# Two mixer networks in one kernel: the last third of every feed-forward made the short one, the handover between phases reordered, and GpSimd's four subtractions merged into one

## The reference, cut to what matters

```python
for l in range(DEPTH):                       # DEPTH = 2
    lat = lat + 0.5 * ml[2] * _swiglu(_modulate(lat, norm_ffn1_g[l], ml[0], ml[1]), *ffn1)
    cx = cx + 0.5 * mc[2] * _swiglu(_modulate(cx, norm_ffn1_g[l], mc[0], mc[1]), *ffn1)
    ... # token mixer on both, residual added
    lat = lat + 0.5 * ml[8] * _swiglu(_modulate(lat, norm_ffn2_g[l], ml[6], ml[7]), *ffn2)
def _swiglu(h, w1, w3, w2):                  # hidden width 2816 = 22 blocks of 128
    return (jax.nn.silu(h @ w1) * (h @ w3)) @ w2
def _modulate(x, g, shift, scale):
    return _rmsnorm(x, g) * (1 + scale) + shift
```

## Time and profile before

| | us |
|---|---|
| median of 3 runs | 2768.28 |
| the profiled execution, its own time | 2765.99 |
| its span, first to last instruction | 2764.2 |
| PE busy | 2650.8 (96%) |
| DVE busy | 1186.9 (43%) |
| ACT busy | 1099.7 (40%) |
| POOL busy | 879.5 (32%) |
| mean granted TensorE clock, share of full speed | 0.977 |

### The profile page before, as it was taken

One profiled execution on the slowest core, in us unless ns is written; L12 is line 12 of the kernel. 1 busy time (PEld: TensorE's weight loads), 2 busy tenths in 40 slices (PEclk: granted clock), 3 DMA queues, 4 the chain that ended last, 5 costly groups with the idle time before them and its releaser, 6 DMA issues. The chain is left out here.

```text
span 2764.2 us, 44695 instructions
## 1 busy us (share of the span) xinstructions
PE 2650.8 (96%) x17377; PEld 2352.3 (85%) x17377; DVE 1186.9 (43%) x1774; ACT 1099.7 (40%) x1517; POOL 879.5 (32%) x1092
## 2 busy tenths in 40 slices
PE   6999999999999999999999999889999999997999
PEld 3777788988888877787877889879999999995999
DVE  3222324226652222252222247654447565634644
ACT  2322333534334222243122247536664554443533
POOL 0222221320013222222222216214544455540554
PEclk8999999999999999999999999999999999997999
DMA  6343542330024344323344334234544345450454
GB/s 236 133 165 131 174 145 92 138 122 16 32 77 160 130 144 152 137 92 137 137 142 147 137 115 154 76 112 151 188 167 150 140 157 188 175 181 16 168 183 152
DMA packets 58503, 376.49 MB, mean 136 GB/s; under 512 B 6223, under 2 KB 12007, under 8 KB 14216
## 3 DMA queue, kind: packets, MB, share of 16 engines
q1 hardware_dynamic: 56988, 371.51, 37.5%
q10 hardware_dynamic: 1388, 3.16, 0.7%
HBM read 370.44 MB, written 3.16 MB: 135 GB/s over the span
## 5 line engine op out<-in xcount | busy, mean ns | idle before, releaser
L1648 POOL TENSOR_TENSOR WL<-RAW,WH 128x256 fp32r<-128x256 f32 x1088 | 879.2, 838 | 1872.3 <-ACT WH L1197 1872.3
L1197 ACT ACTIVATE WH<-RAW 128x1024 fp32r<-128x1024 f32 x544 | 545.7, 1050 | 958.4 <-PE PSA L549 940.7
L1671 DVE TENSOR_TENSOR WL<-RAW,WH 128x1024 fp32r<-128x1024 f32 x272 | 338.2, 1243 | 1139.5 <-ACT WH L1197 1139.4
L547 PE MATMUL PSA<-HH,WH 128*128 128x512 f32 (+1 forms) x1664 | 598.8, 360 | 16.8 <-DVE HL L1756 7.9
L548 PE MATMUL PSA<-HL,WH 128*128 128x512 f32 (+1 forms) x1664 | 589.5, 354 | 0.0
L549 PE MATMUL PSA<-HH,WL 128*128 128x512 f32 (+1 forms) x1664 | 588.7, 354 | 0.0
L547 PE MATMUL PSA<-GH,WH 128*128 128x256 f32 (+1 forms) x1664 | 529.4, 318 | 4.8 <-DVE GL L1689 4.8
L548 PE MATMUL PSA<-GL,WH 128*128 128x256 f32 (+1 forms) x1664 | 521.4, 313 | 0.0
L549 PE MATMUL PSA<-GH,WL 128*128 128x256 f32 (+1 forms) x1664 | 521.0, 313 | 0.0
L547 PEld LDWEIGHTS PSA<-HH,WH 128*128 128x128 f32 x1664 | 316.3, 190 | 75.8 <-issue 25.7
L549 PEld LDWEIGHTS PSA<-HH,WL 128*128 128x128 f32 x1664 | 316.4, 190 | 43.8
(11 more groups left out here) (298 smaller groups left out, 3064.1 us busy)
## 6 DMA issues: line engine op xcount, KB each, us to landing
RAW<-in_weights SPq DMA_DIRECT2D x272, 1024.0 KB, 4.8
ADA<-in_w_ada SPq DMA_DIRECT2D x65, 1024.0 KB, 4.8
Zada<-in_w_ada SPq DMA_DIRECT2D x7, 1024.0 KB, 13.4
scratch_bias<-BREL ACTq DMA_DIRECT2D x1, 2048.0 KB
SUMS<-in_c_sums SPq DMA_DIRECT2D x1, 1664.0 KB, 8.5
TB<-scratch_bias SPq DMA_DIRECT2D x1, 1536.0 KB, 10.8
X<-in_x SPq DMA_DIRECT2D x1, 1024.0 KB, 8.4
X<-in_ctx SPq DMA_DIRECT2D x1, 1024.0 KB, 12.4
```

What stands on the lines that cost most here:

```text
L547: pe.matmul(out, a_hi, b_hi, start=start, stop=False)
L1197: act.activation(WH[:, j, 4 * h:4 * h + 4, :], RAW[:, j, 4 * h:4 * h + 4, :], ACT.Copy)\
L1648: ins = pool.tensor_tensor(WL[:, j, kb, :], RAW[:, j, kb, :], WH[:, j, kb, :].bitcast(F32), ALU.subtract)
L1671: dve.tensor_tensor(WL[:, j, 0:4, :], RAW[:, j, 0:4, :], WH[:, j, 0:4, :].bitcast(F32), ALU.subtract)\
```

## The change

`THIRDS` goes from (8, 6, 8) to (8, 8, 6). The number of slots and of matmuls stays the same; the `down` phase with 6 used blocks is now the last of each feed-forward. In the handover, PE does `part(2, 0)` whole before the column sums of stream 1; ACT splits the first of the next slots ahead of `root(1)`, and the second ahead of `high(1, 0)`; DVE evicts and splits earlier. POOL's four instructions per slot become one of four times the size.

```diff
--- before.py
+++ after.py
@@ -30,7 +30,7 @@
 NL = 256
 FF = 2816
 FFB = FF // P
-THIRDS = (8, 6, 8)
+THIRDS = (8, 8, 6)
 SLOT = KB * 256
 EPS = 1e-6
 NEG = -1.0e30
@@ -652,9 +652,9 @@
             def units_by_stream(ph):
 
                 kin = ph["kin"]
-                def part(u, s, ms=(0, 1)):
+                def part(u, s):
                     j, t = u % 2, streams(512)[s][1]
-                    for m in ms:
+                    for m in range(2):
                         w = slice(P * m, P * m + P)
                         for kb in range(kin):
                             if s == 1 and m == 0:
@@ -672,9 +672,8 @@
                 if has_ada(ph, 1):
                     ada_finish(ph, 1)
                 pe.wait_ge(bank_read[1], 2 + ph["unit"] + BANK_CREDIT)
-                part(2, 0, (0,))
+                part(2, 0).then_inc(mm_done, 1)
                 part_sums(3, 1)
-                part(2, 0, (1,)).then_inc(mm_done, 1)
                 part(3, 0).then_inc(mm_done, 1)
                 part_sums(2, 0)
 
@@ -1236,14 +1235,13 @@
                                        bias=MODS[:, ph["mods"][0], kb, s:s + 1]).then_inc(hh_ready, 1)
                 squares(2, 1)
                 squares(3, 1)
+                after_slot(down, 1, 0, 2)
                 root(1)
-                after_slot(down, 1, 0, 2)
                 squares(2, 0)
-                high(1, range(0, 3))
                 after_slot(down, 1, 1, 2)
-                high(1, range(3, 7))
+                high(1, range(0, 4))
                 squares(3, 0)
-                high(1, range(7, KB))
+                high(1, range(4, KB))
                 root(0)
                 high(0, range(KB))
 
@@ -1644,9 +1642,8 @@
 
             def split_lo(slot, j):
                 pool.wait_ge(hi_ready, slot * 2 + 2)
-                for kb in range(4, KB):
-                    ins = pool.tensor_tensor(WL[:, j, kb, :], RAW[:, j, kb, :], WH[:, j, kb, :].bitcast(F32), ALU.subtract)
-                ins.then_inc(lo_ready[1], 1)
+                pool.tensor_tensor(WL[:, j, 4:8, :], RAW[:, j, 4:8, :], WH[:, j, 4:8, :].bitcast(F32), ALU.subtract)\
+                    .then_inc(lo_ready[1], 1)
 
             for slot in range(2):
                 split_lo(slot, slot)
@@ -1809,21 +1806,22 @@
                 evict(3, 1)
                 n.skip(part_done, 2)
                 modulations()
+                dve.wait_ge(mm_done, down["slot"] + 3)
+                evict(2, 0)
                 mean(1, 8)
+                after_slot(down, 1, 0, 2)
                 dve.wait_ge(gl_ready, n.at(gl_ready))
                 dve.wait_ge(h_ready, hbase)
                 inverse(1)
                 scaled(1, 0)
-                dve.wait_ge(mm_done, down["slot"] + 3)
-                evict(2, 0)
-                after_slot(down, 1, 0, 2)
                 for kb in range(KB):
                     if kb + 1 < KB:
                         scaled(1, kb + 1)
-                    lower(1, kb)
-                    if kb == 4:
+                    if kb == 1:
                         dve.wait_ge(mm_done, down["slot"] + 4)
                         evict(3, 0)
+                    lower(1, kb)
+                    if kb == 1:
                         after_slot(down, 1, 1, 2)
                 mean(0, 4)
                 inverse(0)
```

## The result

| us | before | after |
|---|---|---|
| median of 4 runs each, same chip | 2767.14 (2764.25 to 2771.05) | 2786.7 (2783.75 to 2788.44) |
| the profiled execution, its own time | 2765.99 | 2782.51 |
| its span | 2764.2 | 2780.7 |
| PE busy / DVE busy / POOL busy | 2650.8 / 1186.9 / 879.5 | 2652.1 / 1202.7 / 690.5 |
| mean granted TensorE clock | 0.977 | 0.976 |

The ratio is 1.0065, with a 95% interval of 1.0052 to 1.0078: slower, by less than 1%. That is 19.6 us in the medians, 18.0 by the ratio (14 to 22 by its interval) and 16.5 in the two profiled executions. 2792 had been forecast, 25.2 more by profile. POOL's busy time fell by 21% and the kernel lost time: POOL's length was never what PE waited for, except in one phase.

What follows compares the result with a forecast made beforehand. PE, busy 96% of the span, was taken as the bound, losing time mainly waiting for HL at four handovers. Terms 17.2 + 2 + 3.8 + 3.4 - 3.2 + 2 gave 25.2 us more: 2792, range 2785 to 2799 (wider 2776 to 2804).

Steps and rivals of the forecast that it cites:

- The hold of DVE: Wherever POOL's merged instruction runs: a two-SBUF-input DVE instruction just behind its start waits for all of it, 2.9 us.
- Rival one: Not slower: DVE is not held by a long POOL instruction; first handover HL lasts 0.5 us; 2770, chance 0.10.
- Its length: POOL's merged instruction, per slot: taken as 2.9 us, between 1.23 (DVE's time) and four pieces alone.
- The order at the handover, 17.2: Four handovers: both splits and the merged instruction make stream 1's last HL 4.3 us later each, 17.2 us.
- The clock, 2: Behind the last HL of the handovers: half-slot matmuls at half speed add about 0.5 us each, 2 us (0 to 6).
- THIRDS, nothing: Three handovers: fewer matmuls cover stream 1's first T, but it is ready before ACT can write HH; no cost.
- rival four: Shorter last third alone costs: HL late at three handovers, at most 2 us, inside the range; no separate chance given.
- w_in of layer 1, -3.2: In w_in of layer 1, POOL takes its turn once per slot, so PE's wait for WL goes: -3.2 us.
- ffn2 of layer 1, 3.8: Up-to-down boundaries: POOL holds GL; PE waits 1.2 us at two with 8 blocks, 1.4 more at one with 6.
- Entries of the mixers, 3.4: DVE's T is held by POOL, delaying KE: 2.0 us in layer 1, 1.4 in layer 0; 3.4 us (0 to 4).
- Other dense stretches, 2: At the retention norm, DVE's WL comes late by some us where PE has little in hand: 2 us (0 to 8).
- Rival three: Much slower: clock stays low longer after idling, held DVE work in retention and both w_in costs more; 2806, chance 0.08.

Runs made afterwards that it cites:

- order alone: Only the changed handover order of PE, ACT and DVE, with old THIRDS and POOL's four pieces, against the kernel before: 2775.84 us, ratio 1.0032.
- second split last: Kernel before with ACT's and DVE's share of the second slot's split moved behind all eight HH and HL of stream 1: 2751.41 us, ratio 0.9950.

## Why the prediction came out as it did

The direction, the mechanism and the range were right, 19.6 us against 25.2. That the sum came so near is in part luck: it put 17.2 + 2 of 25.2 on the handovers and too little behind them.

- **The hold of DVE**: right. POOL's 2.35 us kept an HL for 2.27. Rival one, whose test was an HL of 0.5 us, falls by this row. The rule of the Trainium skill (SBUF — State Buffer, "Who interferes with whom"), that the loser is blocked for the whole instruction, agrees with these rows up to 1024 elements.
- **Its length**: 2.9 taken for the merged instruction, 2.5 measured in most slots (2.49 is the median of 272), and 2.35 at the handover. The value lay nearer to the upper bound that I took than to 1.23.
- **The order at the handover, 17.2**: the step that was mis-sized most. First HL forecast for M + 5.65, measured M + 4.9; last HL forecast for M + 13.7, measured M + 12.9, thus 3.5 us later instead of 4.3; POOL's shorter instruction explains 0.55 of the difference. (The first two T were ready at M + 1.6, 1.9 forecast; the table load ahead of them is a row of 1.28 us with no idle time of ACT on either side.) From M to the mean of squares that closes it, the four handovers lasted 3.7, 3.5, 2.2 and 4.2 us longer in the two traces, 13.6 in all, which is what the four last HL, each 3.4 us later, come to. Within a trace the last HL is a fair price in the other kernels too (all four handovers: order alone 10.2 us by the last HL, 9.3 in length; second split last -12.2 and -13.1). The runs find less: the order alone cost 7.9 us, and with the merger at those slots 7.3 (8.3 by the ratio, 5 to 12 by its interval). The 13.6 hold what the clock did in one execution, up to 2.4 us in a handover as shown above, and 3.2 us of the shift went again between handovers 1 and 2, where the kernel with the merger in w_in of layer 1 alone, unchanged there, lost them too. How much of the 13.6 belongs to the change stays open; the runs allow 5 to 12.
- **What the waits tell**: PE's waits for HL rose by 6.4 us in all and not by 14. The view counts too little of what HL costs: at the low clock a block's matmuls fill the time up to the next HL, and the row shows no idle time, but PE still begins each block within 0.2 us of the end of its HL, down to the last:

```profile
463.63 0.48 DVE L1799 SCALAR_TENSOR_TENSOR HL<-T,MODS,HH 128x256 fp32r<-128x256 f32 x1
464.17 0.58 PE L547 MATMUL PSA<-WH,HH 128*128 128x256 f32 x1
...
465.47 0.48 DVE L1799 SCALAR_TENSOR_TENSOR HL<-T,MODS,HH 128x256 fp32r<-128x256 f32 x1
466.00 0.58 PE L547 MATMUL PSA<-WH,HH 128*128 128x256 f32 x1
466.38 0.48 DVE L1799 SCALAR_TENSOR_TENSOR HL<-T,MODS,HH 128x256 fp32r<-128x256 f32 x1
466.92 0.58 PE L547 MATMUL PSA<-WH,HH 128*128 128x256 f32 x1
```

- **The clock, 2**: the low stretch behind the wait is there and longer, 0.50 over 7.2 us. Its price can't be told from the mean: that is 0.977 and 0.976 in the two profiled executions, 0.976 to 0.979 over the runs of the kernel before in the experiments and 0.973 to 0.977 over those of the changed one, and in the attention the profiled execution of before was itself 3.4 us slow.
- **THIRDS, nothing**: right in time, shown alone. In the changed order the reason holds as well: the last HL ends at M + 12.9 with either `kin`. In the old order it does not (M + 11.3 for M + 9.4), which is rival four, and small.
- **w_in of layer 1, -3.2**: wrong in sign. The run with the merger in this phase alone lost 6.4 us. The wait for WL did go (3.2 us), and 4.6 of waiting for ROWS came. The rest goes with the granted clock, which around these waits is 0.87 over 25.5 us where it was 1.00, some 3 us by an estimate (0.13 of 25.5). Before, then after:

```profile
1704.00:1729.50 25.50, 22.32 (x191) 21.20 (x191) 21.54 (x16) 17.66 (x20) 20.93 (x14) 1.00 0.62 238
```

```profile
1717.00:1742.50 25.50, 20.95 (x154) 20.03 (x155) 22.43 (x16) 17.52 (x19) 7.91 (x3) 0.87 0.46 167
```

I looked at POOL's side, which gets its turn once, and not at DVE's, whose queue has a short copy that PE waits for behind its own WL. The rows of the changed kernel, DVE and POOL beside each other:

```profile
1668.37 2.29 DVE L2184 TENSOR_TENSOR Ztm<-LF,Ztm 128x2048 f32<-128x2048 f32 x1
1670.58 3.44 DVE L1668 TENSOR_TENSOR WL<-RAW,WH 128x1024 fp32r<-128x1024 f32 x1
1673.94 0.41 DVE L1682 COPY ROWS<-PSA 128x256 f32<-128x256 f32 x1
...
1668.61 4.33 POOL L1645 TENSOR_TENSOR WL<-RAW,WH 128x1024 fp32r<-128x1024 f32 x1 [9.45 <-ACT WH L1196]
```

POOL was asked at 1668.61, waited 2.05 for DVE's L2184, and then kept DVE's WL (1.23 us of work) until 1672.9, so that it lasted 3.44 and ROWS was copied 2.2 us later. Where PE had nothing in hand it stopped, at two places:

```profile
1718.66 0.38 PE L565 MATMUL PSA<-PR,ROWS 128*128 128x2 f32 x2 [1.70 <-DVE ROWS L1682]
...
1736.44 0.38 PE L565 MATMUL PSA<-PR,ROWS 128*128 128x2 f32 x2 [2.90 <-DVE ROWS L1682]
```

- **ffn2 of layer 1, 3.8**: two boundaries of 8 blocks cost 0.54 and 0.53 instead of 1.2 each, the one of 6 blocks 2.13 instead of 2.5 (before 1.10), and a wait for X of 1.09 went: 1.0 in all, as the shift from behind the mixer to behind ffn2 says (+1.1).
- **Entries of the mixers, 3.4**: right for layer 1 in place and near in size (2.0 forecast), but by another wait. T was held 2.11 us where it takes 0.45, and the wait for GLO rose from 0.8 to 3.4 us; the wait for KE, which the prediction saw growing, fell from 6.5 to 5.6. Not seen in layer 0, where the shift is 3.6 behind the first handover and 0.4 at M of the second (805.22 - 804.79). The rows of layer 1:

```profile
1755.47 2.11 DVE L2227 TENSOR_TENSOR T<-T,Zfm 128x256 f32<-128x256 f32 x1
...
1768.45 0.79 PE L861 MATMUL PSA<-GHI,MEND 128*128 128x512 f32 x1 [3.40 <-DVE GLO L1686]
```

- **Other dense stretches, 2**: low. From behind ffn2 to behind the retention the shift rose by 5.1 to 5.3 us in each kernel of the table with the merger everywhere, and in none of the others. A wait for Z of 1.49, one for SBS of 1.50 and, behind the retention norm, one for GL of 1.48 make up most of it:

```profile
2242.79 3.42 DVE L1668 TENSOR_TENSOR WL<-RAW,WH 128x1024 fp32r<-128x1024 f32 x1
...
2253.83 0.35 PE L547 MATMUL PSA<-GH,WH 128*128 128x256 f32 x1 [1.48 <-DVE GL L1686]
```

These are stops in steady phases, as ROWS in w_in is, and the prediction named such stops as a sign of being wrong. By that sign it was: the forecast had no term for them but the 2 us of this one.

In short: the handovers some 8 us by the runs (5 to 12) and 13.6 in the one pair of traces, instead of 19; what lies behind them 10.5 by the shifts (9.7 to 20.2), and 10 to 12 by the runs (the changed kernel against the one merged at the handovers alone), instead of 6. The two errors had opposite signs, and so the sum was better than its parts. Rival three was right in one part, that w_in would cost; what spoke against it in my text, that PE waits nowhere for DVE there before, was no evidence on what a hold would do.

## What to carry to other kernels

Where a GpSimd instruction and a VectorE instruction with two SBUF operands share time, judge the length of a piece by what stands behind it in VectorE's queue, not by GpSimd's busy time: a quarter as many instructions saved 190 us of POOL's busy time here and cost 15.5 us. Keep bulk work that is not due (here the split of the second slot) behind the short chain that TensorE waits for: moved ahead of it, it was part of the 8 us lost; moved behind, it won 16.6 us (13.9 by the ratio). And don't price a chain by TensorE's counted idle time alone: at the low clock its matmuls fill the time up to the next link, and the idle time grew here by 6.4 us where the last link came 13.7 later in all.

## What the runs showed of the hardware

- One GpSimd subtraction of 128 x 1024 in float32 takes 2.49 us, two of 128 x 512 take 2.64 together and four of 128 x 256 take 2.93 (medians of 272 slots each): 0.15 us for each instruction more.
- Each of the two engines waits for the other's current instruction, in both directions: POOL 2.05 us for a DVE instruction of 2048 elements, DVE 2.2 for POOL's of 1024. DVE's evictions, with one SBUF operand and one from PSUM, kept their time: a pair took 0.86 us beside POOL in the kernel before and 0.87 after POOL's end at the first handover of the changed one.
- The granted clock over a stretch of unchanged work differed between executions (0.80 and 0.83 in the attention, 91.0 and 87.6 us). So did that of one handover with the same instructions (1.00 and 0.76, 11.4 and 13.8 us from M to its closing mean). That is some 3 us of shift in single profiles with no cause in the edit.
